# The long branch's values made with tokens on the partitions, first in each block, and three gate pairs ahead of the branch projections

## The reference, cut to what matters

```python
h = rms_norm(x, norm_g)                       # x: 4096 tokens x 1024
proj = einsum('bsd,de->bse', h, w_in)         # one input projection, 1024 -> 5376
(qa, ka, va, za, qb, kb, vb, zb, ga, gb) = split(proj)
# branch A: 8 query heads on 2 key/value heads, own chunk of 64 and 1 before, rope on q and k, sinks
ya = swa_sink_attention(rope(qa), rope(ka), va, sinks) * silu(za)
# branch B: 8 heads of 64, own chunk of 64 and 8 before, learned relative bias
yb = chunked_relpos_attention(qb, kb, vb, rel_bias) * silu(zb)
merged = sigmoid(ga + bias_a) * (ya @ w_br_a) + sigmoid(gb + bias_b) * (yb @ w_br_b)
out = rms_norm(x + merged @ w_out, final_g)
```

## Time and profile before

| | |
|---|---|
| median of 3 runs | 3460.74 us (3460.51 to 3461.7) |
| the profiled execution's own time | 3458.64 us |
| its span | 3456.8 us |
| PE busy | 3369.6 us, 97% |
| DVE, ACT, POOL busy | 1483.7, 1432.5, 1313.8 us |
| granted TensorE clock, mean | 0.999 |
| DMA, mean over the span | 92 GB/s |

### The profile page before, as it was taken

How to read it: one execution, slowest core, us unless ns; L and a number is a source line. 1 busy time by engine, 2 the same in 40 slices (tenths; PEclk the granted TensorE clock), 3 DMA queues, 4 the chain that set the end, 5 groups by cost and what they waited for, 6 DMA issues and landing times.

```text
span 3456.8 us, 48457 instructions
## 1 busy us (share of the span) xinstructions
PE 3369.6 (97%) x16456; PEld 2502.4 (72%) x16456; DVE 1483.7 (43%) x3113; ACT 1432.5 (41%) x2985; POOL 1313.8 (38%) x1087
## 2 busy tenths in 40 slices
PE   7999999999999999999999999999999999999998
PEld 5667866678666786667866678666786667866686
DVE  5561355513554135541355413554135541355412
ACT  4443344433444334443344434444344443444432
POOL 3334432344323443234532344323443234532244
PEclk9999999999999999999999999999999999999999
DMA  4122421224212242122421124212242112421123
GB/s 145 59 68 87 169 92 50 67 87 165 92 50 67 86 166 92 50 67 86 170 87 54 63 86 171 88 54 62 89 168 92 50 62 92 167 90 49 56 91 116
DMA packets 97788, 319.63 MB, mean 92 GB/s; under 512 B 9984, under 2 KB 26624, under 8 KB 95360
## 3 DMA queue, kind: packets, MB, share of 16 engines
q1 hardware_dynamic: 97536, 316.34, 28.1%
HBM read 299.52 MB, written 16.78 MB: 91 GB/s over the span
## 4 chain that ended last, share of the span: by engine, by line
PE 49%; issue 28%; POOL 13%; DVE 7%; ACT 2%; POOLq 0%; DMA 0%; DVEq 0%; ACTq 0%; SPq 0%
POOL w_lo L746 12%; PE acc L876 10%; PE acc L878 8%; PE acc L877 8%; PE ps_o L969 5%; PE ps_pt L937 4%; PE sc L917 2%; PE sc L908 2%; PE sc L876 1%; PE sc L878 1%; PE sc L877 1%; DVE sc L1212 1%; DVE negm L1220 1%; PE acc L978 1%; DVE probs_t L1286 1%
## 5 line engine op out<-in xcount | busy, mean ns | idle before, releaser
L746 POOL TENSOR_TENSOR w_lo<-w_raw,w_hi 128x512 fp32r<-128x512 f32 x928 | 1211.7, 1311 | 2096.0 <-ACT w_hi L1023 2095.9
L876 PE MATMUL acc<-h_hi,w_hi 128*128 128x512 f32 x2688 | 1117.0, 416 | 16.7 <-DVE q L1273 12.4
L878 PE MATMUL acc<-h_hi,w_lo 128*128 128x512 f32 x2688 | 1054.3, 392 | 0.0
L877 PE MATMUL acc<-h_lo,w_hi 128*128 128x512 f32 x2688 | 1050.8, 391 | 0.0
L1023 ACT ACTIVATE w_hi<-w_raw 128x512 fp32r<-128x512 f32 x928 | 573.5, 624 | 333.8 <-DMA w_raw<-w 104.5
L876 PEld LDWEIGHTS acc<-h_hi,w_hi 128*128 128x128 f32 x2688 | 505.0, 188 | 233.7 <-issue 144.0
L878 PEld LDWEIGHTS acc<-h_hi,w_lo 128*128 128x128 f32 x2688 | 504.9, 188 | 112.6
L877 PEld LDWEIGHTS acc<-h_lo,w_hi 128*128 128x128 f32 x2688 | 506.9, 189 | 83.7
L1105 ACT ACTIVATE probs_b<-sc,negm 128x640 f32<-128x640 f32 x256 | 203.6, 795 | 381.3 <-DVE negm L1220 379.6
L1245 DVE SCALAR_TENSOR_TENSOR part<-th,sc 128x512 f32<-128x512 f32 x64 | 43.9, 686 | 566.5 <-PE sc L878 566.5
L1112 ACT ACTIVATE probs_t<-ps_pt 128x512 f32<-128x512 f32 (+1 forms) x272 | 150.6, 554 | 235.2 <-PE ps_pt L937 235.2
(11 more groups left out here) (119 smaller groups left out, 3566.0 us busy)
## 6 DMA issues: line engine op xcount, KB each, us to landing
w_raw<-w SPq DMA_DIRECT2D x464, 512.0 KB, 3.5
rows<-x SPq DMA_DIRECT2D x36, 512.0 KB, 7.7
xt<-x_t SPq DMA_DIRECT2D x16, 1024.0 KB, 9.9
out<-rows SPq DMA_DIRECT2D x32, 512.0 KB, 2.7
x_in<-x SPq DMA_DIRECT2D x28, 512.0 KB, 5.7
cs<-rope_tab SPq DMA_DIRECT2D x8, 512.0 KB, 4.3
bias<-near SPq DMA_DIRECT2D x1, 1024.0 KB, 13.3
g_out<-final_g SPq DMA_DIRECT2D x1, 512.0 KB, 11.3
```

Of the source, the lines that this page charges most:

```text
L746: pool.tensor_tensor(w_lo[n % 2][:, c], w_raw[n % 2][:, c], w_hi[n % 2][:, c].bitcast(FP32), ALU.subtract).then_inc(w_split, 1)
L876: pe.matmul(dst[:, :], hi, src_hi[:, k, :], start=begin, stop=False)
L877: pe.matmul(dst[:, :], hi, src_lo[:, k, :], start=False, stop=False)
L878: mm = pe.matmul(dst[:, :], lo, src_hi[:, k, :], start=False, stop=end)
```

## The change

The 512 value channels of branch B are no longer made as four tiles v4 to v7 with channels on the partitions. Four new tiles, `vt`, hold the same weights as two row groups of 128 x 512 each. They stand first in the block. `value_columns` makes their products with the activations as PE's loaded weights and the weight tile streaming through, into four banks: two of `sc0`, `ps_o` and `acc1`. A step `v_out` behind them has ACT copy two banks and DVE two, straight into `v_b`. The turns of v4 to v7 are gone; that of `v0` stays, now directly behind `v0`'s last quarter. The lead grows from 24 to 36 quarters; the order of the other tiles changes (z0 goes from the lead into `fill`, k4 stands ahead of q4, and in `fill` the q tiles of branch A come at other beats). `AHEAD` goes from 2 to 3, so `fill` now has 94 quarters: 17 tiles from z0 to z7, three gate pairs, and the first two quarters of `br0`. `turned` and `spread` now lie on the buffers `part` and `whole`. The diff without its context lines:

```diff
@@ -91,8 +91,8 @@
-    names = "k0 v0 q0 z0 q4 k4 v4 z4 q1 z1 q5 k5 v5 z5 q2 z2 q6 k6 v6 z6 q3 z3 q7 k7 v7 z7"
-    tiles = [(t[0], int(t[1])) for t in names.split()]
+    names = "k0 q0 v0 k4 q4 z0 q1 z4 k5 q5 z1 q2 z5 k6 q6 z2 q3 z6 k7 q7 z3 z7"
+    tiles = [("vt", kk) for kk in range(O_TILES)] + [(t[0], int(t[1])) for t in names.split()]
@@ -102,13 +102,14 @@
-AHEAD = 2
+AHEAD = 3
+HALVES = 2
+O_TILES = KT // HALVES
+V_BANK = 1
 NORMED_AT = 18
-HALVES = 2
-O_TILES = KT // HALVES
@@ -146,12 +147,14 @@
-    v, z, k4 = tile("v", 0), tile("z", 0), tile("k", 4)
-    lead = [*tile("k", 0), v[0], [*v[1], ("rope_in_k", 0)], v[2], [("rope_k", 0), *v[3]],
-            *tile("q", 0), [*z[0], ("turn_v", 0)], [*z[1], ("rope_in", 0)], z[2], [("rope", 0), *z[3]],
-            *tile("q", 4), k4[0], k4[1], k4[2], k4[3]]
+    q, v, k4 = tile("q", 0), tile("v", 0), tile("k", 4)
+    lead = [[("mm", n, c)] for n in range(O_TILES) for c in range(QUARTERS)]
+    lead[0] = [("claim_v",), *lead[0]]
+    lead[-1] = [*lead[-1], ("v_out",)]
+    lead += [*tile("k", 0), q[0], [*q[1], ("rope_in_k", 0)], q[2], [("rope_k", 0), *q[3]],
+             v[0], [*v[1], ("rope_in", 0)], v[2], [("rope", 0), *v[3]], [("turn_v", 0), *k4[0]], *k4[1:], *tile("q", 4)]
     for t in range(TT):
-        at_ = 18 + t
+        at_ = QUARTERS * O_TILES + 14 + t
@@ -160,14 +163,12 @@
-    fill = tiles(("v", 4), ("gb", AHEAD - 1))
-    first_fill = TILES.index(("v", 4))
+    fill = tiles(("z", 0), ("gb", AHEAD - 1))
+    first_fill = TILES.index(("z", 0))
         at_ = QUARTERS * (i - first_fill + 1)
-        if name == "v":
-            fill[at_ + 1] = [("turn_v", s), *fill[at_ + 1]]
-        elif name == "q" and s < PAIRS:
+        if name == "q" and s < PAIRS:
@@ -287,7 +288,7 @@
     for step in PLAN:
-        if step[0] == "mm" and TILES[step[1]][0] not in ("br", "o"):
+        if step[0] == "mm" and TILES[step[1]][0] not in ("br", "o", "vt"):
@@ -297,6 +298,8 @@
             job_, bank_ = step, step[1]
+        elif step[0] == "claim_v":
+            job_, bank_ = step, V_BANK
@@ -413,12 +416,14 @@
     cs = sb("cs", [P, 2, BLK])
-    turned = sb("turned", [P, BLK])
-    spread = sb("spread", [P, TT, P])
     gate = sb("gate", [P, BLK])
+    part_at = off[0]
     part = sb("part", [P, BLK])
+    turned = at("turned", [P, BLK], FP32, part_at)
+    whole_at = off[0]
     whole = sb("whole", [P, BLK])
+    spread = at("spread", [P, TT, P], FP32, whole_at)
@@ -447,7 +452,7 @@
               (acc[0][:, :], acc[1][:, :], sc[1][:, 0, :], sc[1][:, 1, :]))
+    ps_v = (sc[0][:, 0, :], sc[0][:, 1, :], ps_o[:, :], acc[V_BANK][:, :])
@@ -468,6 +473,8 @@
     o_used = sem("o_used")
+    v_used = sem("v_used")
+    v_out = [sem("v_out_act"), sem("v_out_dve")]
@@ -589,6 +596,8 @@
             eng.wait_ge(w_half_used, b * NEARLY + (sum(early_half(i) for i in range(n)) + 1))
+        elif name == "vt":
+            eng.wait_ge(v_used, b * O_TILES + (idx + 1))
@@ -849,9 +858,35 @@
+            def value_columns(b, first, n, c):
+                kk = TILES[n][1]
+                if c % 2 == 0:
+                    pe.wait_ge(w_split, b * (2 * NW) + (2 * n + c // 2 + 1))
+                    pe.wait_ge(h_done, b * KT + (2 * kk + c // 2 + 1))
+                if n == 0 and c == 0 and not first:
+                    pe.wait_ge(rows_added, (b - 1) * ADDED + TT)
+                j = c // 2
+                k = 2 * kk + j
+                for t in (2 * (c % 2), 2 * (c % 2) + 1):
+                    dst = ps_v[t]
+                    h_h, h_l = h_hi[:, k, t * P:(t + 1) * P], h_lo[:, k, t * P:(t + 1) * P]
+                    hi = w_hi[n % 2][:, j * BLK:(j + 1) * BLK]
+                    lo = w_lo[n % 2][:, j * BLK:(j + 1) * BLK]
+                    pe.matmul(dst, h_h, hi, start=k == 0, stop=False)
+                    pe.matmul(dst, h_h, lo, start=False, stop=False)
+                    mm = pe.matmul(dst, h_l, hi, start=False, stop=k == KT - 1)
+                if c == 1:
+                    mm.then_inc(w_half_used, 1)
+                elif c == QUARTERS - 1:
+                    mm.then_inc(v_used, 1)
                 name, idx = TILES[n]
+                if name == "vt":
+                    value_columns(b, first, n, c)
+                    return
@@ -862,8 +897,6 @@
                     pe.wait_ge(w_split, b * (2 * NW) + (2 * n + c // 2 + 1))
-                if n == 0:
-                    pe.wait_ge(h_done, b * KT + 2 * (c + 1))
@@ -888,6 +921,9 @@
                     pe.wait_ge(probs_ready, b * NUNIT + free_from)
+                if n == 0 and t == 0:
+                    for engine in range(2):
+                        pe.wait_ge(v_out[engine], (2 - engine) * b + (2 - engine))
@@ -947,12 +983,11 @@
                         wait_freed(pe, b, ("turn_v", 0))
-                        if not first:
-                            wait_kept(pe, b, "keep_v", PAIRS - 1)
                     else:
-                        wait_freed(pe, b, ("turn_v", s))
-                        if not first:
-                            wait_kept(pe, b, "keep_v", s)
+                        for engine in range(2):
+                            pe.wait_ge(v_out[engine], (2 - engine) * b + (2 - engine))
+                    if not first:
+                        wait_kept(pe, b, "keep_v", max(s, PAIRS - 1))
@@ -1002,7 +1037,7 @@
                         turn_four(b, step, part)
-                    elif kind == "claim_o":
+                    elif kind in ("claim_o", "claim_v"):
@@ -1088,6 +1123,12 @@
                             split_hi(b, n, half)
+                    elif kind == "v_out":
+                        act.wait_ge(v_used, (b + 1) * O_TILES)
+                        if not first:
+                            wait_kept(act, b, "keep_v", SETS - 1)
+                        for t in (0, 2):
+                            act.activation(v_b[:, TT + t, :], ps_v[t], ACT.Copy).then_inc(v_out[0], 1)
@@ -1140,6 +1181,8 @@
                 dve.wait_ge(x_rstd, b + 1)
+                if not (isinstance(b, int) and b == 0):
+                    dve.wait_ge(m_done, b * KT)
@@ -1285,13 +1328,17 @@
                     elif kind == "turn_v":
-                        s = step[1]
                         if not first:
-                            wait_kept(dve, b, "keep_v", max(s, PAIRS - 1))
-                        c = (s - PAIRS) * P
-                        dst = v_a[:, 1:1 + TT, :] if s == 0 else v_b[:, TT:2 * TT, c:c + P]
-                        dve.tensor_copy(dst, bank(step)[:, :].rearrange("p (t c) -> p t c", t=TT)).then_inc(free(step), 1)
+                            wait_kept(dve, b, "keep_v", PAIRS - 1)
+                        dve.tensor_copy(v_a[:, 1:1 + TT, :],
+                                        bank(step)[:, :].rearrange("p (t c) -> p t c", t=TT)).then_inc(free(step), 1)
+                    elif kind == "v_out":
+                        dve.wait_ge(v_used, (b + 1) * O_TILES)
+                        if not first:
+                            wait_kept(dve, b, "keep_v", SETS - 1)
+                        dve.tensor_copy(v_b[:, TT + 3, :], ps_v[3]).then_inc(free(("claim_v",)), 1)
+                        dve.tensor_copy(v_b[:, TT + 1, :], ps_v[1]).then_inc(v_out[1], 1)
@@ -1394,6 +1441,10 @@
     for name, n in TILES:
+        if name == "vt":
+            m = w_in[0][2 * n * P:2 * (n + 1) * P, starts["vb"]:starts["vb"] + BLK]
+            tiles.append(m.reshape(2, P, BLK).transpose(1, 0, 2).reshape(P, KT * P))
+            continue
```

## The result

Before and after ran in turn on one chip, four times each: 3461.07 us (3460.51 to 3461.7) before, **3421.22 us** (3420.73 to 3422.05) after; ratio 0.9887, 95% interval 0.9874 to 0.99. The forecast of 3435 had the sign and left out a third of the gain: 39.9 us where I said 26. The time lies under the forecast's own range (3424 to 3445) and inside the 8 in 10 range (3416 to 3452). The profiled execution took 3421.02 us, its span is 3419.2 (37.6 less) and the mean granted clock is 0.999, as before.

What follows compares the result with a forecast made beforehand. PE's stream, busy 97%, was taken as the bound. Seven blocks at -2.9 (-20.3) and block 0 at -5.5 gave -25.8: 3435 us, own range 3424 to 3445, 8 in 10 range 3416 to 3452.

Steps and rivals of the forecast that it cites:

- What bounds the kernel: PE, busy 97% of the span: its stream is the time, shortened only by fewer instructions or shorter stalls.
- vt products at 0.227, 0 us: In the lead, vt tiles replace v4 to v7 with equally many products at 0.227 us each: no change.
- Turns, -1.8 a block: Removed turns of v4 to v7: four a block, each 0.45 us of PE with its restart.
- full-price rival: Each of 128 removed transposes saves its full 0.272 us, 34.8 in all: 3415 us; chance 0.03.
- Lead waits -3.2, turn of v0 +1.0: In the lead, DVE's row work no longer delays q0's rope, -3.2; v0's turn newly waits for ACT's copy, +1.0.
- Ropes in the A sets, +3.4 a block: Ropes of q1, q2, q3 meet DVE's score shaping or gate in A sets: waits of 0.7, 1.9 and 0.8 us.
- Ropes out of the B sets, -2.3 a block: B sets lose 0.9 us each to late copies of turned probabilities; without ropes this goes, half in the third.
- The last set's end, 0: Waits around T10, V6 and br0 at the end of the last set: -0.5 to 0, taken as 0.
- The start, -4.6 once: Program start: 1.55 us won by an earlier first product, 3.1 by k0's rope no longer waiting for DVE's constants.
- Block 0's sets, -1.9: Block 0's sets: removed turns -1.8, B sets -3.5 in place of -2.3, ropes in A sets +3.4.
- a sign against it: Waits at a block's first matmul, for the banks of the last block's rows, would show the forecast wrong.

Runs made afterwards that it cites:

- double_turn: Changed kernel with the norm's four transposes made twice in each A set: 3432.71 us, ratio 0.9921 to the kernel before.
- turn_later: Changed kernel with the turn of v0 one quarter later, behind k4's first quarter: 3414.48 us, ratio 0.9867 to the kernel before.
- finish_late: Changed kernel with squares, finishing and storing of the last block's rows 12 quarters later: 3452.32 us, ratio 0.998 to the kernel before.
- ropes_in_b: Changed kernel with fill's tiles reordered so the ropes of q1, q2 and q3 fall in the B sets again: 3415.33 us, ratio 0.9869.
- one_turn: Kernel before with one of four transposes of each of v4 to v7, copies kept: 3460.12 us, ratio 1.0002.
- claim_later: Changed kernel with the wait for acc1 one quarter later, ahead of the first product writing it: 3419.81 us, ratio 0.9881.
- ahead2: Changed kernel with two gate pairs ahead instead of three, and eight empty beats in fill: 3480.52 us, ratio 1.0062 to the kernel before.

## Why the prediction was right in direction and short in size

- *What bounds the kernel*: held. Each us gained is a removed turn or a shorter stall of PE. What left ACT and DVE is in no term of it; where their operations stand in their queues is in most.
- *vt products at 0.227, 0 us*: held (1271.92 to 1303.00).
- *Turns, -1.8 a block*: held. In block 3 six products, a turn and six products took 3.31 us before, and twelve products take 2.86 now: 0.45. A4, which has no rope in either kernel, is 0.48 shorter. *double_turn* gives 0.44 for four more transposes away from any wait. The full-price rival (3415) is nearer to the measured time than the forecast is, and refuted all the same.
- *Lead waits -3.2, turn of v0 +1.0*: -2.2 forecast, -2.4 measured in block 3. *turn_later* shows the second part (0.95). *finish_late* shows that the first hangs on where the rows are finished, but gives back 3.9 and not 3.2, since there the rows stand at other ropes than before. (q0's rope comes 12 quarters later, the 28th of the lead and not the 16th, and not the 14 that I wrote; no term hangs on it.)
- *Ropes in the A sets, +3.4 a block*: held in the seven blocks. In block 3 it is 0.69 at q1, 1.85 at q2, 0.82 at q3 with their restarts, 3.4 together; for q2, q1 and q3 1.9, 0.7 and 0.8 was the forecast. The sets' lengths against *ropes_in_b* give 3.7. q1's place in the timeline after:

```profile
1349.64 0.54 PE L953 MATMUL sc<-k_b,q 64*128 64x320 f32 x2 [0.26 <-ACT probs_b L1146]
...
1354.74 0.50 PE L909 MATMUL acc<-h_hi,w_hi 128*128 128x512 f32 x1 [0.30 <-DVE q L1316]
```

- *Ropes out of the B sets, -2.3 a block*: about -2.7, which is what the sets' length leaves once the other terms are taken (-1.69 less -1.8 + 3.4 - 0.6). The table says the same: B1, B2 and B3 are 1.61, 1.55 and 1.14 shorter, 0.5 of each the permutations, so -2.8. Of the three B sets only the third, with its z job, still waits for a copy (timeline of PE):

```profile
1483.98 0.55 PE L973 MATMUL ps_pt<-ident,probs_b 128*128 128x128 f32 x3 [0.18 <-DVE probs_t L1329]
```

- *The last set's end, 0*: it was -0.6. From T9's start to the third quarter of `br0` 11.98 us before hold five quarters, 5.17 beside them; 5.91 after hold one, 4.55 beside it. The waits are 0.36 and 0.77 where they were 0.20 and 1.50:

```profile
1555.49 0.33 PE L973 MATMUL ps_pt<-ident,probs_b 128*128 128x128 f32 x1 [0.36 <-DVE probs_t L1329]
...
1557.62 0.69 DVE L1366 TENSOR_TENSOR whole<-ps_o,gate 128x512 f32<-128x512 f32 x1 [2.19 <-PE ps_o L1004]
```

I had -0.5 as the outcome of the working and took 0.
- *The start, -4.6 once*: a wrong size, by a wrong reading. The first product came at 16.37 (16.1 forecast). But before, the second tile began at 25.94, not at the 27.1 that I put there. In the timeline after:

```profile
16.37 0.76 PE L876 MATMUL sc<-w_hi,h_hi 128*128 128x512 f32 x1 [2.38 <-DVE h_lo L1199]
...
24.44 1.27 POOL L755 TENSOR_TENSOR w_lo<-w_raw,w_hi 128x512 fp32r<-128x512 f32 x1 [10.57 <-ACT w_hi L1058]
...
25.76 0.50 PE L876 MATMUL sc<-w_hi,h_hi 128*128 128x512 f32 x1 [1.37 <-POOL w_lo L755]
```

The early start is spent waiting for `w_lo`, and 0.2 us are won there and not 1.55. It was worth less than its 1.07 us anyway: in both kernels the first products start 0.43 us apart, and 0.23 only from about 21.5 on. The lead of block 0 won 2.3, and I had 3.6 for it.
- *Block 0's sets, -1.9*: the largest miss of one term, they won 7.0. Its B sets took 24.12, 24.16 and 24.11 us before and 21.35, 21.38 and 21.70 after; less the 1.5 of permutations that moved, that is -6.5 where I had -3.5. Its A sites cost 2.3 and not 3.4 (q1's wait isn't there), and its end gave 1.0. *ropes_in_b* gives 3.1 of the 7.0 back in these sets, so that much is the order of the tiles; the turns (1.8) and the end (1.0) are two further parts, and about 1 us has no place.

Sum: of the 11.8 us of span that the forecast lacks, 3.9 are in block 0 and 8.1 in the others (28.4 for 20.3), less the 0.2 ahead of PE's first instruction. Per block of the seven that is 1.15 on average, of which the end of the last set is 0.6 and the B sets 0.4.

**What stays open.** Block 3 pays 0.87 us at the next block's first product, for the last block's rows, as the prediction named for a sign against it; two other starts show 0.51 and 0.42 with no releaser, the rest none. They speak less against the prediction than it said, for they are not the change's alone: *one_turn*, which has the order of the kernel before, shows 0.63, 0.19 and 0.94 at three starts, and in the variants of the kernel after they stand at other blocks and differ in size from run to run (a wait on `rows` of 0.92 at block 2 in *finish_late*, of 1.00 at block 6 in *turn_later*). *claim_later* moved one of the two possible causes, the claim of `acc1`, and changed nothing beyond the noise. The other, the wait on the rows themselves, can't be taken away without a race on their banks and wasn't tried; nor was the loop's turn-round separated from it. The blocks without that wait won up to 1.0 more than block 3's terms sum to, and that remainder has no place.

## What to carry to other kernels

Charge a removed instruction at the distance between starts, with its restart, and then look for the next claim of the same bank: work taken off an engine that arrives early at a claim is handed back as waiting (*one_turn*). Where a step is moved, list every reader of every bank that its neighbours take, and each one's place in its engine's queue; the three bad places here (the turn, q2's tile, q3's `rope_in`) cost 21 us together and were repaired by moving single steps by one quarter or one tile. Write each start and end of the sum from a row: the one time that I inferred (27.1) was wrong by 1.2 us. And look at the granted clock before a longer time is put down to the waits: by the estimate above a third of what *ahead2* lost came with a clock that fell behind them.

## What the runs showed that I had not expected

- Removed transposes buy nothing while the bank that they write is still copied late: 96 less, ratio 1.0002.
- Four transposes of 0.27 us duration take 0.35 us of the stream and eight 0.79, 0.10 each.
- In *ahead2* the granted clock was down at half behind a row of waits of about 1 us, in the last set of all eight blocks: an estimated 20 of its 59 us.
- Single repairs add up: four of them, 6.7, 1.4, 5.9 and 8.5 us alone, give 23 together.
